# Differential attention: score operands widened to 128 rows, units in three-bank runs two deep, one maximum instruction per unit

## The reference, cut to what matters

```
s = einsum('bhcqd,bhckd->bhcqk', q_blk, k_all) * scale   # c = 0, 1; d = 64
p = softmax(s)
a = p[:, :, 0] - lam * p[:, :, 1]
out = einsum('bhqk,bhkd->bhqd', a, v_all)
```

## Time and profile before

| | |
|---|---|
| runs | 2960.71 us median of 3 (2959.38 to 2961.1) |
| profiled execution | 2964.78 us, span 2963.0 us |
| TensorE busy | 2695.5 us (91%) |
| VectorE busy | 1494.3 us (50%) |
| ScalarE busy | 769.1 us (26%) |
| GpSimd busy | 723.5 us (24%) |
| attention, layer 1 | 272.5 to 438.0 us of the span |
| attention, layer 2 | 1334.0 to 1474.2 us |
| attention, layer 3 | 2369.0 to 2470.5 us |

### The profile page before, as it was taken

How to read it: one execution, slowest core, us unless ns; L and a number is a source line. 1 busy time by engine, 2 the same in 40 slices (tenths; PEclk the granted TensorE clock), 3 DMA queues, 4 the chain that set the end, 5 groups by cost and what they waited for, 6 DMA issues and landing times.

```text
span 2963.0 us, 29738 instructions
## 1 busy us (share of the span) xinstructions
PE 2695.5 (91%) x12765; PEld 2101.9 (71%) x12765; DVE 1494.3 (50%) x1737; ACT 769.1 (26%) x1023; POOL 723.5 (24%) x218
## 2 busy tenths in 40 slices
PE   7998889799999997998879999979979998899997
PEld 3787447688888886794467778767967636677876
DVE  3994645655644445855447655651038432524323
ACT  2223433221111112323332122123132233312212
POOL 1113001122222222311022334323323001333431
PEclk9987768899999998996788999988986898899998
DMA  7222002234333331211022445432200200222331
GB/s 246 86 93 79 0 4 69 71 107 121 107 115 102 118 104 53 90 60 66 0 57 78 136 141 167 146 93 72 71 29 1 65 0 20 66 88 83 97 96 50
DMA packets 309220, 240.52 MB, mean 81 GB/s; under 512 B 10692, under 2 KB 304831, under 8 KB 309087
## 3 DMA queue, kind: packets, MB, share of 16 engines
q1 hardware_dynamic: 308674, 238.47, 26.3%
q10 hardware_dynamic: 414, 0.13, 0.0%
HBM read 232.29 MB, written 2.10 MB: 79 GB/s over the span
## 4 chain that ended last, share of the span: by engine, by line
PE 78%; DVE 14%; ACT 5%; issue 2%; DMA 1%; POOL 0%; DVEq 0%; SPq 0%; ACTq 0%
PE ps L1930 55%; PE ps L636 5%; PE ps L1943 4%; PE ps L663 3%; PE ps L651 2%; DVE hid_lo L1841 2%; PE ps L585 2%; PE ps L1904 2%; DVE n_wide L1560 1%; DVE xg L1600 1%; DVE conv_acc L770 1%; DVE h_lo L1587 1%; DVE mod_w L1623 1%; DVE mod_ctx L1623 1%; ACT probs L691 1%
## 5 line engine op out<-in xcount | busy, mean ns | idle before, releaser
L1211 POOL TENSOR_TENSOR w_lo<-raw,w_hi 128x2048 fp32r<-128x2048 f32 (+2 forms) x160 | 658.6, 4116 | 2109.3 <-ACT w_hi L1298 2109.3
L1930 PE MATMUL ps<-h_hi,w_hi 128*128 128x512 f32 x2288 | 750.3, 374 | 48.4 <-DVE h_lo L1587 35.8
L1930 PE MATMUL ps<-h_lo,w_hi 128*128 128x512 f32 x2288 | 740.2, 370 | 0.0
L1930 PE MATMUL ps<-h_hi,w_lo 128*128 128x512 f32 x2288 | 738.3, 369 | 0.0
L1298 ACT ACTIVATE w_hi<-raw 128x2048 fp32r<-128x2048 f32 (+2 forms) x160 | 274.7, 1717 | 890.4 <-PE ps L1930 606.6
L1930 PEld LDWEIGHTS ps<-h_hi,w_hi 128*128 128x128 f32 x2288 | 393.5, 192 | 146.3 <-DVE h_lo L1587 36.6
L1930 PEld LDWEIGHTS ps<-h_hi,w_lo 128*128 128x128 f32 x2288 | 393.8, 192 | 77.9
L1930 PEld LDWEIGHTS ps<-h_lo,w_hi 128*128 128x128 f32 x2288 | 395.0, 192 | 74.6
L1841 DVE TENSOR_TENSOR hid_lo<-sq,hid_hi 128x512 fp32r<-128x512 f32 (+1 forms) x66 | 276.3, 4186 | 90.9 <-ACT hid_hi L1517 90.9
L1930 PE MATMUL ps<-hid_hi,w_hi 128*128 128x512 f32 x704 | 237.7, 378 | 26.8 <-DVE hid_lo L1841 26.8
L1930 PE MATMUL ps<-hid_lo,w_hi 128*128 128x512 f32 x704 | 234.7, 374 | 0.0
(11 more groups left out here) (289 smaller groups left out, 2723.9 us busy)
## 6 DMA issues: line engine op xcount, KB each, us to landing
mod_w<-in_w_mod SPq DMA_DIRECT2D x72, 1024.0 KB, 8.9
raw<-in_w_ffn_in SPq DMA_DIRECT2D x88, 512.0 KB, 5.2
raw<-in_w_in SPq DMA_DIRECT2D x54, 512.0 KB, 4.7
raw<-in_w_ffn_out SPq DMA_DIRECT2D x48, 384.0 KB, 3.8
raw<-in_w_out SPq DMA_DIRECT2D x24, 512.0 KB, 4.7
raw<-in_w_gate SPq DMA_DIRECT2D x22, 512.0 KB, 4.0
raw<-in_w_up SPq DMA_DIRECT2D x22, 512.0 KB, 5.3
raw<-in_w_down SPq DMA_DIRECT2D x24, 384.0 KB, 3.5
```

What stands on the lines that cost most here:

```text
L1211: pool.tensor_tensor(w_lo[:, s, 0:floats], raw[:, s, 0:floats], w_hi[:, s, 0:floats].bitcast(F32), ALU.subtract).then_inc(lo_ready, 1)
L1930: ins = pe.matmul(ps[0:m, at:at + tw], w[:, k, cols], v[:, k, t0:t0 + tw], start=(at_k == 0 and j == 0), stop=(at_k == k_tiles - 1 and j = ...
```

## The change

In layers 1 and 2 `double_pe`, `double_act` and `double_dve` take the place of the three attention functions; layer 3 keeps these.

- Scores have operands of 128 rows. For the first pair, rows 64 to 127 of the queries in `qk` are zeroed. For the second, a copy of rows 64 to 127 is made in another buffer (`q_other`, in `qk_swap` or `qk_sq`) whose rows 0 to 63 are zeroed. Keys are read with all 128 rows. VectorE makes this (`pad`): heads 0 and 1 before the key multiplications, heads 2 and 3 in the background of unit 1.
- Both pairs of a unit lie side by side in a run of 1536 columns, with the products cut at bank edges, and there are two such runs. A unit's scores wait for the exponentials of the unit two before it. One maximum instruction reads both pairs, one multiply follows.
- All six transposes have columns of their own from 3072; the last two lie in the bank of V's product and wait for its save.
- The order on each engine is rewritten, and is seen at the end of each function.
- Layer 3's context is no longer turned before layer 2's attention but behind the products of layer 2's output blocks 0 and 1, into the free columns of their slot, and copied by VectorE before it adds the block. SP's wait before the modulation pair is now for output block 1.

```diff
+        def CTX2_AT(n, half):
+            return 2048 * (n % 2) + 1024 * half + 512
...
                 if l == 1 and layers == 3:
-                    sp.wait_ge(xt_done, XT_STEPS + 4)
+                    sp.wait_ge(gemm_done, base_out[1] + 2)
                 load_pairs_after(base_out[l] + 3)
...
+        swap_flat = qk_swap[:, :, :, :].rearrange("p a b c -> p (a b c)")
+        def q_other(h):
+            return swap_flat[:, TOK * h:TOK * h + TOK] if h < 2 else qk_sq[:, h - 2, :]
+        def double_at(u, v, c):
+            return 1536 * (u % 2) + v["nk"] * c
+        def double_pe(pe, l, values):
+            us = units[l]
+            def score(u):
+                v = us[u]
+                h, nk = v["h"], v["nk"]
+                if u == 0 or us[u - 1]["h"] != h:
+                    pe.wait_ge(p_done, 4 * l + h + 1)
+                    pe.wait_ge(q_pad, 2 * l + h // 2 + 1)
+                if u >= 2:
+                    pe.wait_ge(at_exp, comp_base[l] + 2 * u - 2)
+                for c, q in ((0, qk[:, h, :]), (1, q_other(h))):
+                    at, k0 = double_at(u, v, c), 0
+                    while k0 < nk:
+                        kw = min(nk - k0, 512 - (at + k0) % 512)
+                        ins = pe.matmul(ps[:, at + k0:at + k0 + kw], q[:, v["q"]:v["q"] + P],
+                                        qk[:, 4 + h, v["k0"] + k0:v["k0"] + k0 + kw], start=True, stop=True)
+                        k0 += kw
+                ins.then_inc(at_s, 2)
+            def turn(u):
+                pe.wait_ge(at_a, unit_base[l] + u + 1)
+                if turn_number(l, u):
+                    pe.wait_ge(at_copied, turn_number(l, u))
+                for step, (first, end) in enumerate(turn_steps(us[u])):
+                    if step and pv_number(l, u):
+                        pe.wait_ge(at_saved, pv_number(l, u))
+                    for k in range(first, end):
+                        at = TURN_AT + P * k
+                        ins = pe.transpose(ps[:, at:at + P], probs[:, u % 2, 0, P * k:P * k + P], ident)
+                    ins.then_inc(at_t, 1)
+            def times_v(u):
+                if not us[u]["last"]:
+                    return
+                j, nk = pv_number(l, u), us[u]["nk"] // P
+                pe.wait_ge(at_copied, turn_number(l, u + 1))
+                if j:
+                    pe.wait_ge(at_saved, j)
+                gw = us[u]["gw"]
+                for k in range(nk):
+                    ins = pe.matmul(ps[:, PV_AT:PV_AT + gw], values(us[u]["k0"] // P + k, us[u]["h"]), probs_t[:, k, 0:gw],
+                                    start=(k == 0), stop=(k == nk - 1))
+                ins.then_inc(at_pv, 1)
+            score(0)
+            score(1)
+            for u in range(len(us)):
+                if u + 2 < len(us):
+                    score(u + 2)
+                if u:
+                    times_v(u - 1)
+                turn(u)
+            times_v(len(us) - 1)
...
+            def exponentials(u):
+                v = us[u]
+                act.wait_ge(at_max, comp_base[l] + 2 * u + 2)
+                if u >= 2:
+                    act.wait_ge(at_t, turn_number(l, u - 1))
...
+            def copy_turned(u):
+                if us[u]["i"] == 0 and pv_number(l, u):
+                    act.wait_ge(at_pv, pv_number(l, u))
...
+            exponentials(0)
+            for u in range(len(us)):
+                if u + 1 < len(us):
+                    exponentials(u + 1)
+                if u:
+                    save(u - 1)
+                copy_turned(u)
+            save(len(us) - 1)
+        def double_dve(dve, l, link, background):
+            us = units[l]
+            def top(u):
+                v = us[u]
+                dve.wait_ge(at_s, comp_base[l] + 2 * u + 2)
+                at, tops = double_at(u, v, 0), small[:, u % 2, 0:2]
+                link(dve.tensor_reduce(tops, ps[:, at:at + 2 * v["nk"]].rearrange("p (c k) -> p c k", c=2), AXX, ALU.max,
+                                       negate=True))
+                dve.tensor_tensor(tops, tops, qk_root[:, v["h"], v["q"] // P, :], ALU.mult).then_inc(at_max, 2)
+            def combine(u):
+                nk = us[u]["nk"]
+                e0, e1, sm = probs[:, u % 2, 0, 0:nk], probs[:, u % 2, 1, 0:nk], small[:, u % 2, :]
+                dve.wait_ge(at_exp, comp_base[l] + 2 * u + 2)
+                link(dve.reciprocal(sm[:, 4:6], sm[:, 2:4]))
+                link(dve.tensor_scalar(e1, e1, sm[:, 5:6], lam[:, l:l + 1], ALU.mult, ALU.mult))
+                dve.scalar_tensor_tensor(e0, e0, sm[:, 4:5], e1, ALU.mult, ALU.subtract).then_inc(at_a, 1)
+            top(0)
+            top(1)
+            for u in range(len(us)):
+                combine(u)
+                background(u)
+                if u + 2 < len(us):
+                    top(u + 2)
...
+                    def pad(j):
+                        for b in range(2 * j, 2 * j + 2):
+                            dve.tensor_copy(q_other(b)[DH:P, 0:T], qk[DH:P, b, 0:T])
+                            ins = dve.memset(q_other(b)[0:DH, 0:T], 0.0)
+                        link(ins)
+                        dve.memset(qk[DH:P, 2 * j:2 * j + 2, 0:T], 0.0).then_inc(q_pad, 1)
                     for j in range(2, 4):
...
+                    dve.wait_ge(p_rot, 4 * l + 4)
+                    for j in range(2):
+                        n = base_in[l] + 4 + j
+                        dve.wait_ge(psum_free[n % 2], n // 2 + 1)
+                    pad(0)
                     for i in range(4, 8):
                         finish_k(i)
...
                     def background(u):
+                        if u == 1:
+                            pad(1)
...
                             window_means()
...
-                    if l == 1 and layers == 3:
-                        for s in range(4):
-                            tt, half = s // 2, s % 2
-                            dve.wait_ge(xt_done, XT_STEPS + s + 1)
-                            dve.tensor_copy(x[:, 4 * half:4 * half + 4, LAT + tt * P:LAT + (tt + 1) * P],
-                                            ps[:, 2048 + 512 * s:2560 + 512 * s].rearrange("p (k t) -> p k t", t=P)
-                                            ).then_inc(x_ready, 1)
-                    attention_dve(dve, l, link, background)
+                    double_dve(dve, l, link, background)
...
                     dve.wait_ge(gemm_done, n + 1)
...
+                    if l == 1 and layers == 3 and b < 2:
+                        for half in range(2):
+                            dve.tensor_copy(x[:, 4 * half:4 * half + 4, LAT + b * P:LAT + (b + 1) * P],
+                                            ps[:, CTX2_AT(n, half):CTX2_AT(n, half) + 512].rearrange("p (k t) -> p k t", t=P))
...
                     add_to_x(n, b, l, 16, parts[l])
...
                     pe.wait_ge(p_rot, 4 * l + 4)
-                    pe.wait_ge(p_done, 4 * l + 4)
-                    def scores(u, c):
-                        return [(qk[64 * c:64 * c + 64, u["h"], u["q"]:u["q"] + P],
-                                 lambda k0, kw: qk[64 * c:64 * c + 64, 4 + u["h"], k0:k0 + kw])]
-                    if l == 1 and layers == 3:
-                        pe.wait_ge(ctx2_landed, 16)
-                        for s in range(4):
-                            for k in range(4):
-                                f = (4 * (s % 2) + k) * P
-                                ins = pe.transpose(ps[:, 2048 + 512 * s + P * k:2048 + 512 * s + P * k + P],
-                                                   ctx2_in[:, s // 2, f:f + P], ident)
-                            ins.then_inc(xt_done, 1)
-                        pe.wait_ge(x_ready, XT_STEPS + 4)
-                    attention_pe(pe, l, scores, lambda kt, h: v_nat[:, kt, h * P:h * P + P])
+                    double_pe(pe, l, lambda kt, h: v_nat[:, kt, h * P:h * P + P])
...
+                def turn_ctx2(n, b):
+                    pe.wait_ge(ctx2_landed, 16)
+                    for half in range(2):
+                        for k in range(4):
+                            f = (4 * half + k) * P
+                            ins = pe.transpose(ps[:, CTX2_AT(n, half) + P * k:CTX2_AT(n, half) + P * k + P],
+                                               ctx2_in[:, b, f:f + P], ident)
+                    return ins
                 for b in range(4):
...
                     block_ready(n, n % 2, n // 2)
+                    then = (lambda: turn_ctx2(n, b)) if l == 1 and layers == 3 and b < 2 else block_pair(n)
                     products(n % 2, KD, 256, parts[l], h_hi, h_lo,
-                             (lambda k: pe.wait_ge(m_lo, 8 * l + k + 1)) if b == 0 else None, block_pair(n),
+                             (lambda k: pe.wait_ge(m_lo, 8 * l + k + 1)) if b == 0 else None, then,
                              MIX_ORDER if l < 2 else None)
...
```

(29 more changed lines are left out.)

## The result

The changed kernel takes 2888.77 us (median of 4, 2882.28 to 2895.51) beside 2960.05 (median of 4) of the kernel before on the same chip: ratio 0.9761, interval 0.9735 to 0.9787. It is 71 us faster; forecast were 66 and 2895 us. Two more measurements of it gave 0.9752 and 0.9736. The profiled execution took 2891.82 us, 73.0 less than that of before.

What follows compares the result with a forecast made beforehand. TensorE at its low clock level was taken to bound the attentions of layers 1 and 2, VectorE next. Gains of 28 + 38 = 66 us off 2964.8 give 2898.8; that execution being 4.1 above the median, 2895 us, range 2872 to 2915.

Steps and rivals of the forecast that it cites:

- TensorE is bound by its low level, and 64-row scores cause it: Attentions of layers 1 and 2: TensorE limits at the 1.2 GHz level; 128-row work precedes its rise, 64-row work its fall.
- TensorE's step, 3.86 us: A 768-key unit's scores and transposes on TensorE: 2.96 + 0.53 + 0.37 us at the high level, 7.38 at the low.
- VectorE's step: A 768-key unit on VectorE: maximum with multiply 1.95 plus combining 2.0, 3.95 us; 4.7 with a piece of modulation work.
- The step with V, 9.3 us: A head's V step on TensorE: 2.96 + 5.3 + 0.9 + 0.2 = 9.3 us, with VectorE working beside it.
- Layer 2: 42.8 less 2 and 3, 38: Layer 2's attention: gain 42.8 us, less 2 for moved context transposes and 3 for falling clock, net 38.
- The moved start: Layer 2's scores no longer wait for the context's DMA and transposes; they start at 1333.8, first turn 1346.5 instead of 1349.45.
- Layer 1: 34 less 6, 28: Layer 1's attention: ends at 404.0 against 438.0, gain 34 us, less 6 for slow clock after three waits, net 28.
- Paddings: VectorE's padding: heads 0 and 1 (4.1 us) free before key multiplications; heads 2 and 3 cost 4.1 and 2.8 us.
- SP's wait, nothing: Moving SP's wait to output block 1 of layer 2 costs nothing, or 0 to 3 us if two more blocks don't cover it.
- Always low, zeros count nothing: Rival, chance 0.08: zero halves count for nothing, so the attentions' clock stays low; 68 us more, 3028 us.
- Clock half kept: Rival, chance 0.17: the clock falls wherever TensorE waits for VectorE, a third of 40 units run low; 2925 us.
- Rows don't matter to the clock: Rival, chance 0.07: the attentions' clock stays at 0.67, only TensorE's gaps shrink; about 10 us less, 2951.

Runs made afterwards that it cites:

- the last experiment but one: Changed kernel with modulation steps before attention, padding and window means behind V, plus GpSimd's window sums held back until three units are combined: 2873.11 us, ratio 0.9684.

## Why the prediction was right

*TensorE is bound by its low level, and 64-row scores cause it.* The first half is right, and so is the remedy: width alone lifts the clock from 0.50 to 0.97 in the same 29 us, and without the width the changed kernel has 0.70 and 0.74. The reading that the clock falls under more 64-row scores is not borne out: with the new order it is 1.00 for 50 us of them. The prediction weighed the Trainium skill, *TensorE: Matmul & The Clock Gate*, "What's actually happening", by which how busy the engine has been decides. These runs contradict it for this kernel: busy 100% gave 0.50 and busy 80% gave 0.97.

*TensorE's step, 3.86 us.* 2.58 + 0.88 = 3.46. The scores were priced at 2.96 from two runs of four; a run of eight takes 2.58. The low step, 7.38, measured 6.89 with 64-row scores.

*VectorE's step.* One maximum was given 1.75 us and takes 1.75, in these groups of the changed kernel in layer 1's attention (line, shapes, count, then busy us, mean ns, idle before):

```profile
L877 DVE TENSOR_REDUCE small<-ps 128x2 f32<-128x1536 f32 x16 | 28.1, 1753 | 23.0 <-PE ps L789 23.0
...
L879 DVE TENSOR_TENSOR small<-small,qk_root 128x2 f32<-128x2 f32 x24 | 7.9, 329 | 2.5
```

The small operations on the chain take 0.16 and 0.09, not 0.2, so the step is 3.78 for 3.95. With modulation it is 4.44 for 4.7, since a piece adds 0.66. The mean of 0.33 us of the multiplies holds the slow ones beside GpSimd.

*The step with V, 9.3 us:* 8.9. *The wait for ScalarE's save, 0.2:* the two transposes follow the save by 0.04 us, and TensorE idles for 0.25, since most of the 0.61 us copy lies beside the first four.

*Layer 2: 42.8 less 2 and 3, 38.* Measured 6.7 + 32.3 less 1.75 in the output blocks (two groups of eight transposes at 0.87): 37.3. Its parts were off and cancelled, which is luck. From the first scores on 97.6 us were given and 101.7 taken. The way to the first turn was given 12.7 us (1333.8 to 1346.5) and took 16.3 (1298.39 to 1314.7): the sum had one unit's scores in it, but the third unit's stand before the first turn in TensorE's queue, at the low level, 5.50 us as at 281.92. The next three turns took 17.6 for 14.6, with a padding of 3.4 for 2.8 and a unit at the low level behind it. The three heads then took 58.5 for 63.5, and the end 9.3 for 6.8, since its transposes and V product ran at the low level (1.54 and 7.36 us). The 3 us set aside for the clock cover most of the sum of these. In the execution that took 98.0 us the way to the first turn was 13.4. The window means of layer 2, 3.1 us, stand in no sum; they fell beside V (1355.9 to 1359.0) and cost nothing.

The moved start was credited with its full earlier beginning. That credit was right in place (2.7 us for 9.4) and worth little or nothing in the sum, as the kernel with the context first shows: what it saves before the scores it loses in good part to GpSimd's sums and to the transposes later.

*Layer 1: 34 less 6, 28.* Measured 36.3, the largest miss. The way to the first turn took 16.3 us for 14.4, again for the third unit's scores; from there to turn 18 it is 92.3 for 97.6, of which the 16 steps with modulation account for 16 x 0.26 = 4; the end 20.4 for 19.5. The 6 us for a falling clock were too much. Products at the low level behind the waits for padding and window means lie mostly beside VectorE, which sets the step, so they cost little there; in the way to the first turn, where TensorE is on the chain, they do cost (4.30 us for a unit's scores, priced at 2.96). The mean clock of 0.91 itself is above the 0.8 named; layer 2's 0.89 is just below its 0.9.

*Paddings.* Of heads 0 and 1, free: right. VectorE makes them at 239.77 to 244.4 and is then idle for 7.67 us before the next key multiplication. Of heads 2 and 3, 4.1 and 2.8: durations 4.7 and 3.4, near; their effect was under-priced. 6.9 us were in the sum, leaving them out gives 9.4 in the attentions and 14.7 by the medians.

*SP's wait, nothing:* the stretch behind layer 2's pool product is 1.0 us longer to the end, less than the 1.75 us of the transposes in it, so nothing shows of that wait.

*The rivals.* "Always low, zeros count nothing" fell by the clocks of 0.91 and 0.89 with zeros. "Clock half kept" fell by the same. "Rows don't matter to the clock" fell by the kernel with width alone, and it was mis-sized: it gave the change without the clock 10 us, and all but the width gave 42. The gaps alone were counted there, not the 0.5 us that each large unit loses between two runs of scores and two of transposes, nor that the new order keeps the high level in layer 2 from the first V product to 1420.

*The range.* Its upper end, 2915, is more than the terms beside it: 3.1 for the paddings, 9 for the clock and 3 for SP's wait are 15 us above 2895, so 2910.

*The forecast's attribution.* The prediction tells nearly the whole gain as a clock story. The runs say: width alone 28 us, all but the width 42, each with its padding paid, and together 71. That the forecast came out at 66 is in part luck: order and width both lead to the same VectorE-bound steps, so a sum that gives all of it to the clock ends at nearly the same time.

## What to carry to other kernels

Where TensorE is busy without a gap at the 1.2 GHz level and its products use half of the rows, fill the other half with zeros and look at the clock; then expect the next engine's loop to take over, and change the order with it, since either alone gave 28 and 42 of 71 us. Measure the order without the width too, as it can keep the clock high by itself. Put VectorE's side work beside the steps in which TensorE has most to do: three moved pieces gave another 16 us here, and one 4.7 us piece in the wrong place made a 2.7 us wait of TensorE one of 7.5. Before crediting an earlier start, ask what other engine's work it now runs beside.

## What the runs showed of the hardware

- Runs of 64-row float32 scores between transposes left TensorE's clock at 0.50 with 29.0 of 29.0 us busy; the same scores with 128 rows, half of them zero, had 0.97 in the same 29 us. With zeros or ones the attentions of the changed kernel have 0.89 to 0.91.
- Lifted by twelve 128-row records times V, the clock stayed at 1.00 for 50 us of 64-row scores, transposes and V products, with waits of at most 0.38 us between them, and was low behind a wait of 3.15. Both are from the kernel with all but the width.
- The same kernel's first scores behind the same 2.73 us wait ran at the low level in two profiled executions (2.90 us for four records) and at the high one in a third (1.53).
- Eight score records of one unit take 2.58 us at the high level with 128 rows and 2.77 with 64, from start to the next start. At the low level they take 5.50 with 128 rows, to their end, and 5.42 with 64; two runs of four with 64 rows and transposes between them take 5.72. So width costs no time.
- A VectorE multiply of two columns from SBUF took 2.62 us instead of 0.16 and ended with GpSimd's 128x1594 sum; the maximum that reads PSUM took 1.77 beside 1.75. The Trainium skill, *SBUF — State Buffer*, "SBUF: two separate sides", says that VectorE operations with two SBUF inputs and GpSimd's take turns at a shared port, and that one waits for the other's whole instruction. The rows agree: the multiply reads two tensors in SBUF, and so does the combination that took 2.14 us for 1.02 in the last experiment but one. The scaling that took 3.21 us for 0.68 there reads only one; the section says the same of operations in a two-port mode, and no row tells whether the scaling ran in one.
- VectorE fills 64x768 float32 in 0.70 us, and copies as much in 0.56.
